# Attention by pairs of heads in column and row halves of TensorE's array, with four score banks and two banks for the turned probabilities

## The reference, cut to what matters

```python
def softmax_attend(q, k, v, scale):
    s = jnp.einsum('bqhd,bkhd->bhqk', q, k, preferred_element_type=jnp.float32) * scale
    p = jax.nn.softmax(s, axis=-1).astype(v.dtype)
    return jnp.einsum('bhqk,bkhd->bqhd', p, v)
```

## Time and profile before

| | |
|---|---|
| median of 3 runs | 2400.22 us (2400.1 to 2400.34) |
| the profiled execution's own time | 2396.24 us |
| its span | 2394.4 us |
| PE busy with matmuls | 2138.0 us (89% of the span) |
| PE busy with weight loads | 1714.3 us |
| DVE busy | 1188.7 us |
| ACT busy | 857.6 us |
| mean granted clock of TensorE | 0.944 of full speed |
| scores L1130 | 192 PE instructions, of 96 matmuls |
| turns L1139 | 320 PE instructions |
| values L1152 | 320 PE instructions, of 160 matmuls |

### The profile page before, as it was taken

The page is one execution under the profiler, slowest core; times in us unless marked ns, Lnnn a source line. Parts: engine busy times, 40 slices in busy tenths (PEclk is TensorE's granted clock), DMA queues, the critical chain, the costliest instruction groups (busy, mean ns, idle before and its releaser), DMA issues.

```text
span 2394.4 us, 32007 instructions
## 1 busy us (share of the span) xinstructions
PE 2138.0 (89%) x12456; PEld 1714.3 (72%) x12456; DVE 1188.7 (50%) x2027; ACT 857.6 (36%) x1362; POOL 188.9 (8%) x186
## 2 busy tenths in 40 slices
PE   4999899799989999998898989889987579986998
PEld 2777458347757777775874746879977579986997
DVE  5322444454454333334433464655667576666665
ACT  3422342253242222222433434343344633333343
POOL 0000000000110003003000000200330320011001
PEclk8999899899999999998998989989989889998998
DMA  8426104012534554545381322855541345542553
GB/s 287 138 80 200 53 18 152 11 53 88 176 105 159 172 180 141 199 151 175 117 261 53 124 58 76 272 187 182 181 140 62 115 131 165 180 159 88 168 184 106
DMA packets 280855, 332.06 MB, mean 139 GB/s; under 512 B 13286, under 2 KB 229788, under 8 KB 280604
## 3 DMA queue, kind: packets, MB, share of 16 engines
q1 hardware_dynamic: 268704, 323.05, 41.3%
q10 hardware_dynamic: 12028, 7.31, 1.2%
HBM read 329.29 MB, written 1.05 MB: 138 GB/s over the span
## 4 chain that ended last, share of the span: by engine, by line
PE 70%; issue 10%; DVE 10%; ACT 4%; DMA 3%; POOL 2%; ACTq 0%; POOLq 0%; DVEq 0%
PE ps L467 17%; PE ps L468 17%; PE ps L469 17%; PE ps L1152 3%; PE ps L344 3%; PE ps L1130 2%; DVE SL L431 2%; PE ps L1139 1%; ACT SH L425 1%; DVE SM L1223 1%; PE ps L354 1%; PE ps L1299 1%; DVE RSTD L839 1%; PE ps L1305 1%; DMA RAW<-in_ffn_w 1%
## 5 line engine op out<-in xcount | busy, mean ns | idle before, releaser
L431 DVE TENSOR_TENSOR SL<-RAW,SH 128x1024 fp32r<-128x1024 f32 (+3 forms) x460 | 530.8, 1157 | 899.8 <-ACT SH L425 897.8
L425 ACT ACTIVATE SH<-RAW 128x1024 fp32r<-128x1024 f32 (+3 forms) x460 | 447.8, 980 | 1067.7 <-PE ps L469 920.6
L467 PE MATMUL ps<-AH,SH 128*128 128x256 f32 (+1 forms) x2048 | 674.1, 329 | 79.3 <-DVE AL L871 30.3
L468 PE MATMUL ps<-AL,SH 128*128 128x256 f32 (+1 forms) x2048 | 665.7, 325 | 0.0
L469 PE MATMUL ps<-AH,SL 128*128 128x256 f32 (+1 forms) x2048 | 664.7, 325 | 0.0
L467 PEld LDWEIGHTS ps<-AH,SH 128*128 128x128 f32 x2048 | 399.2, 195 | 143.7 <-issue 49.4
L469 PEld LDWEIGHTS ps<-AH,SL 128*128 128x128 f32 x2048 | 398.9, 195 | 29.3
L468 PEld LDWEIGHTS ps<-AL,SH 128*128 128x128 f32 x2048 | 399.3, 195 | 27.3
L467 PE MATMUL ps<-HH,SH 128*128 128x256 f32 (+1 forms) x992 | 310.1, 313 | 8.2 <-DVE HL L741 4.4
L469 PE MATMUL ps<-HH,SL 128*128 128x256 f32 (+1 forms) x992 | 309.0, 311 | 0.0
L468 PE MATMUL ps<-HL,SH 128*128 128x256 f32 (+1 forms) x992 | 308.2, 311 | 0.0
(11 more groups left out here) (237 smaller groups left out, 2207.6 us busy)
## 6 DMA issues: line engine op xcount, KB each, us to landing
SIDE<-in_w_mod SPq DMA_DIRECT2D x45, 2048.0 KB, 8.1
RAW<-in_ffn_w SPq DMA_DIRECT2D x64, 1024.0 KB, 5.4
RAW<-in_w_in SPq DMA_DIRECT2D x44, 1024.0 KB, 5.8
RAW<-in_w_ffn_gate SPq DMA_DIRECT2D x22, 1024.0 KB, 10.1
RAW<-in_w_ffn_up SPq DMA_DIRECT2D x22, 1024.0 KB, 5.9
RAW<-in_w_ffn_down SPq DMA_DIRECT2D x16, 1024.0 KB, 5.6
RAW<-in_w_branch SPq DMA_DIRECT2D x24, 512.0 KB, 3.5
RAW<-in_w_out SPq DMA_DIRECT2D x8, 1024.0 KB, 5.5
```

What stands on the lines that cost most here:

```text
L425: e.activation(SH[:, m, 0:kt, :], RAW[p][:, 0:kt, o:o + P], ACT.Copy).then_inc(K.up("weight_high"), 1)
L431: e.tensor_tensor(SL[:, m, 0:kt, :], RAW[p][:, 0:kt, o:o + P], SH[:, m, 0:kt, :].bitcast(F32), ALU.subtract).then_inc(K.up("weight_low"), 1)
L467: e.matmul(ps, SH[:, m, k, :], xh, start=k == 0, stop=False)
L468: e.matmul(ps, SH[:, m, k, :], xl, start=False, stop=False)
```

## The change

- The steps are put in another order: the two heads of a pair alternate, so that step n and step n+1 (n even) are the same query tile of an even and of an odd head. In `na` their scores then lie in the upper and in the lower 64 rows of the array.
- Scores use four banks, ps6, ps7, ps2 and ps3 (columns of SM for maxima and sums are also four deep). Turns use two banks, ps5 and ps1. Outputs of values use ps4 and ps0 in turn, one for each pair of heads.
- The values are computed once for four steps: for each 128 keys, one matmul of the even head into the partitions 0 to 63 and one of the odd head into the partitions 64 to 127 of the same bank.
- The orders on PE, ACT and DVE are rewritten in twos, as below. The scaling of the probabilities stays on DVE and stays in place.
- The section waits at its start for all eight banks, and the sections behind it wait for its last readers of all eight.

The number of instructions of each kind is unchanged. The diff, cut to its core:

```diff
+        SCORES = (6, 7, 2, 3)
+        TURNED = (5, 1)
+        OUT = (4, 0)
-            self.steps = [(s, h, qt) for s in range(streams) for h in range(HEADS) for qt in range(2)]
+            self.steps = [(s, 2 * hp + j, qt) for s in range(streams) for hp in range(HEADS // 2) for qt in range(2)
+                          for j in range(2)]
+            self.pairs = len(self.steps) // 4
...
-            for b in (4, 5, 6, 7):
+            for b in range(8):
                 reader, count = K.bank[b]
                 e.wait_ge(sem[reader], K.value(reader, count))
...
             def scores(n):
-                if n >= 2:
-                    e.wait_ge(sem["exp_done"], K.at("exp_done", n - 1))
+                if n >= 4:
+                    e.wait_ge(sem["exp_done"], K.at("exp_done", n - 3))
...
             def turn(n):
                 e.wait_ge(sem["probs_ready"], K.at("probs_ready", n + 1))
-                if n:
-                    e.wait_ge(sem["turned_copied"], K.at("turned_copied", n))
+                if n >= 2:
+                    e.wait_ge(sem["turned_copied"], K.at("turned_copied", n - 1))
...
+            def values(pair):
+                s, h, _ = self.steps[4 * pair]
+                e.wait_ge(sem["turned_copied"], K.at("turned_copied", 4 * pair + 4))
+                if pair >= 2:
+                    e.wait_ge(sem["branch_low"], K.at("branch_low", pair - 1))
+                o = PS[self.OUT[pair % 2]]
                 for j in range(tiles):
-                    ins = e.matmul(o, V[:, c0 // P + j, 64 * h:64 * h + 64], PTS[:, g % 2, j, :], start=j == 0,
-                                   stop=j == tiles - 1)
+                    for i in range(2):
+                        ins = e.matmul(o[64 * i:64 * i + 64, 0:256], V[:, c0 // P + j, 64 * (h + i):64 * (h + i) + 64],
+                                       PTS[:, i, j, :], start=j == 0, stop=j == tiles - 1)
...
-            scores(0)
-            scores(1)
-            for n in range(n_steps):
-                if n + 2 < n_steps:
-                    scores(n + 2)
+            for n in range(4):
+                scores(n)
+            for n in range(0, n_steps, 2):
                 turn(n)
-                if n >= 2 and n % 2 == 0:
-                    values(n // 2 - 1)
-            values(n_steps // 2 - 1)
-            K.bank[4] = ("branch_low", K.s("branch_low") + n_steps // 4)
-            K.bank[5] = ("turned_copied", K.s("turned_copied") + n_steps)
-            K.bank[6] = K.bank[7] = ("exp_done", K.s("exp_done") + n_steps)
+                turn(n + 1)
+                if n >= 4 and n % 4 == 0:
+                    values(n // 4 - 1)
+                if n + 4 < n_steps:
+                    scores(n + 4)
+                    scores(n + 5)
+            values(self.pairs - 1)
+            for b in self.OUT:
+                K.bank[b] = ("branch_low", K.s("branch_low") + self.pairs)
+            for b in self.TURNED:
+                K.bank[b] = ("turned_copied", K.s("turned_copied") + n_steps)
+            for b in self.SCORES:
+                K.bank[b] = ("exp_done", K.s("exp_done") + n_steps)
...
         def act(self, e, K):
-            for n in range(n_steps + 1):
+            for n in range(0, n_steps + 2, 2):
                 if n < n_steps:
                     exp(n)
-                if n >= 1:
+                    exp(n + 1)
+                if n >= 2:
+                    turned(n - 2)
                     turned(n - 1)
-                if n >= 5 and (n - 5) % 4 == 0:
-                    out((n - 5) // 4)
+                if n >= 6 and n % 4 == 2:
+                    out((n - 6) // 4)
...
         def dve(self, e, K):
-            for n in range(n_steps + 1):
+            for n in range(n_steps + 2):
                 if n < n_steps:
                     maximum(n)
-                if n >= 1:
-                    normalise(n - 1)
-                if n >= 6 and (n - 6) % 4 == 0:
-                    out((n - 6) // 4)
+                if n >= 2:
+                    normalise(n - 2)
+                if n >= 9 and n % 4 == 1:
+                    out((n - 9) // 4)
```

More of the change, by code:

```diff
@@ L1110, in qk, with scores_of @@
             return Q96[0:96, h, q0:q0 + P], K96[0:96, h, c0:c1]
+        def scores_of(self, n):
+            c0, c1 = self.keys(self.steps[n][0])
+            return PS[self.SCORES[n % 4]][:, 0:c1 - c0]
         def pe(self, e, K):
@@ L1125, in scores @@
                 s, h, qt = self.steps[n]
-                if n >= 2:
-                    e.wait_ge(sem["exp_done"], K.at("exp_done", n - 1))
-                q, k = self.qk(s, h, qt)
-                c0, c1 = self.keys(s)
[L1130 to L1135, removed]
-                if n:
-                    e.wait_ge(sem["turned_copied"], K.at("turned_copied", n))
-                for j in range((c1 - c0) // P):
-                    ins = e.transpose(PS[5][:, j * P:(j + 1) * P], PR[:, n % 2, j * P:(j + 1) * P], IDENT)
-                ins.then_inc(K.up("probs_turned"), 1)
@@ L1142, in values @@
[L1142 to L1147, removed]
+                if n >= 4:
+                    e.wait_ge(sem["exp_done"], K.at("exp_done", n - 3))
+                q, k = self.qk(s, h, qt)
+                e.matmul(self.scores_of(n), q, k, start=True, stop=True).then_inc(K.up("scores_done"), 1)
@@ new lines, in turn @@
+            def turn(n):
+                c0, c1 = self.keys(self.steps[n][0])
+                e.wait_ge(sem["probs_ready"], K.at("probs_ready", n + 1))
+                if n >= 2:
+                    e.wait_ge(sem["turned_copied"], K.at("turned_copied", n - 1))
+                for j in range((c1 - c0) // P):
+                    ins = e.transpose(PS[self.TURNED[n % 2]][:, j * P:(j + 1) * P], PR[:, n % 2, j * P:(j + 1) * P],
+                                      IDENT)
+                ins.then_inc(K.up("probs_turned"), 1)
@@ L1169, in outputs @@
+            for b in self.TURNED:
+                K.bank[b] = ("turned_copied", K.s("turned_copied") + n_steps)
+            for b in self.SCORES:
+                K.bank[b] = ("exp_done", K.s("exp_done") + n_steps)
         def outputs(self, pair):
             s = self.steps[4 * pair][0]
-            return pair % 4, slice(s * SEQ, (s + 1) * SEQ), slice(256 * (pair % 2), 256 * (pair % 2) + 256)
+            return pair % 4, slice(s * SEQ, (s + 1) * SEQ), PS[self.OUT[pair % 2]][:, 0:256]
         def act(self, e, K):
@@ L1176, in exp @@
             def exp(n):
-                s, h, qt = self.steps[n]
-                c0, c1 = self.keys(s)
+                c0, c1 = self.keys(self.steps[n][0])
                 e.wait_ge(sem["max_done"], K.at("max_done", n + 1))
@@ L1181, in exp @@
                     e.wait_ge(sem["probs_turned"], K.at("probs_turned", n - 1))
-                e.activation(PR[:, n % 2, 0:c1 - c0], PS[6 + n % 2][:, 0:c1 - c0], ACT.Exp,
-                             bias=SM[:, n % 2:n % 2 + 1], accum_out=SM[:, 2 + n % 2:3 + n % 2]) \
-                    .then_inc(K.up("exp_done"), 1)
+                e.activation(PR[:, n % 2, 0:c1 - c0], self.scores_of(n), ACT.Exp, bias=SM[:, n % 4:n % 4 + 1],
+                             accum_out=SM[:, 4 + n % 4:5 + n % 4]).then_inc(K.up("exp_done"), 1)
             def turned(n):
@@ L1214, in maximum @@
                 s, h, qt = self.steps[n]
-                c0, c1 = self.keys(s)
                 e.wait_ge(sem["scores_done"], K.at("scores_done", n + 1))
-                ps = PS[6 + n % 2]
+                ps = self.scores_of(n)
                 if self.kind == "na" and s == 0:
```

37 lines of the change are left out of this document (18 added, 19 removed).

## The result

The changed kernel takes 2434.72 us (median of 4 runs, 2427.44 to 2443.25), against 2400.16 us (4 runs, 2398.88 to 2400.34) for the kernel before, run beside it. The ratio is 1.0142, with a 95% interval from 1.012 to 1.0163: slower by 1.4%. The forecast was 2443 us with a range from 2409 to 2484.

A forecast was written before the change was run, and what follows sets the result against it. PE was taken to bound the kernel before. Stage changes of +43 us took the profiled 2396.24 us to 2439; the runs' median stands 4 us above, giving 2443 us, range 2409 to 2484.

The forecast's parts named there:

- The circle: Attention: DVE waits for scores queued behind turns and values; `na` pair, 512 keys, 2.4 GHz, 12.31 us against 10.86.
- The halves: Values in Attention: column halves overlap, so a pair's 16 instructions take 1.87 us; bounds 1.87 to 3.74.
- Row halves: Scores of two heads in `na`: may overlap, bounds 0 to 0.86 us for a pair of scores; nothing counted.
- The clock: `na` mostly at 1.2 GHz, priced 14 to 46 us; `mla` at 2.4 GHz except part of the 256-key steps.
- the first rival: Attention: the ring of waits closes but the clock stays up; +3.5 us, 2404 us, chance 0.14.
- The third case: `mla` loses its clock too: pairs of 14.6 instead of 9.9 us, 2478 us in all, chance 0.15.
- The sum: Four attention stages: `na` +26.5 and +15, `mla` +1.1 and -1.4, +2 for low clock; in all +43 us.
- The 2 us for the unit behind each `na`: After each `na`: the unit behind starts at the low clock, plus 2 us in each layer.
- The rises of the clock: `na`: a short rise after each run of values, worth 0.8 us each; -2.5 in layer 0, -1.5 in layer 1.
- a shorter tail: End of each attention: one run of values in halves instead of two whole ones, -1.9 us with 512 keys.
- The handover wait: End of each attention: the next unit's first matmul waits in ps0 for YH and YL, about 0.95 us, four times.
- The rival on the other side: Attention: DVE or PE work is the bound, not the ring of waits; faster, 2331 us, chance 0.05.

The follow-up runs named there:

- kernel with fillers: Changed kernel plus one unread score matmul on PE ahead of each turn, in both attentions; 2417.34 us, ratio 1.0079 against the kernel before.
- kernel with swapped outputs: Changed kernel with the two output banks of the values, ps4 and ps0, exchanged; 2434.46 us, ratio 1.013 against the kernel before.
- the one with the filler in `na` alone: Changed kernel plus unread score matmuls ahead of turns, only in `na` and from the second two steps on; 2422.61 us, ratio 1.0086.
- both handover edits: Changed kernel with the two output banks exchanged and ps0 counted free after the last pair but one; 2434.18 us, ratio 1.0136.
- scores-first kernel: Changed kernel with the scores of steps n+4 and n+5 put ahead of turns n and n+1; 2354.81 us, ratio 0.9813 against the kernel before.
- the halves in series: Values of one head issued whole before the other's: 2448.53 us in the changed kernel, 2372.91 us with the scores also ahead of the turns.
- the old queues and new values: Changed kernel with PE, ACT and DVE orders of the kernel before, keeping new head order, banks and column halves; 2378.59 us, ratio 0.9919.

## Why the prediction was right, and where it was off

**What bounds the kernel.** PE bound the kernel before and was no longer the bound after, as forecast: its busy share in the first `na` fell from 95 to 70%, the wait of DVE for the score stands in every second step (3.21 us at 1.2 GHz, 1.61 in `mla`), and the turn waits for the scaling.

**The circle.** Its sums for 512 keys, and for 256 at the low clock, held; each is made of differences in the timeline of before:

| two steps, us | predicted | measured | where |
|---|---|---|---|
| `na` 512 keys, 2.4 GHz | 5.22 and 7.09 with values | 5.21 and 7.09 | kernel with fillers |
| `na` 512 keys, 1.2 GHz | 6.64 and 10.24, less 0.8 for a rise | 6.62 and 9.28 | 275.66, 282.28, 291.56 |
| `na` 256 keys, 1.2 GHz | 3.7 and 5.6 | 3.60 and 5.51 | waits of L1236 at 340.98, 344.58, 350.09 |
| `mla` 512 keys, 2.4 GHz | 4.08 and 6.17 | 4.09 and 6.15 | 515.05 to 525.29 |

For the third line, the maxima that waited for a score of 256 keys:

```profile
340.98 0.42 DVE L1236 TENSOR_REDUCE SM<-ps 128x1 f32<-128x256 f32 x1 [3.84 <-PE ps L1138]
344.58 0.42 DVE L1236 TENSOR_REDUCE SM<-ps 128x1 f32<-128x256 f32 x1 [1.60 <-PE ps L1138]
350.09 0.42 DVE L1236 TENSOR_REDUCE SM<-ps 128x1 f32<-128x256 f32 x1 [3.84 <-PE ps L1138]
```

For 256 keys at 2.4 GHz the sum was 2.90 us, and 3.91 with values. `mla` shows 2.64 (553.20 to 555.84) and 3.85 (563.47 to 567.32), and once 4.99, where the clock was 0.66 (555.84 to 560.83). The 2.90 had been made from rows of `na`.

**The halves.** Taken as 1.87 us for 16 instructions, from a row with column quarters; measured 1.95 with the tail of the last, as 8 had 1.94. Right.

**Row halves.** I counted nothing for them. They overlap (last section). In the changed kernel I see no gain from it, for the reason given: DVE needs the second score later, and the first of each two comes no sooner (280.17 to 282.28 is 2.11 us, as in the earlier trace rows). No run took the overlap away, so this is read from the timeline and not tested.

**The clock.** Taken as mostly 1.2 GHz in `na`: 0.59 and 0.61 are right, against the first rival. For `mla` I took 2.4 GHz but for part of the 256-key steps: 0.98 and 1.00 in this execution. The third case (`mla` loses its clock too) is not borne out by this execution: `mla` has as many turns as `na` and kept its clock. The Trainium skill's rule on transposes that stood beside it (TensorE: Matmul & The Clock Gate, PE-mode transpose) therefore does not decide here: 96 transposes in each of the two stages, 0.59 in the one and 0.98 in the other. But the case is not quite dead either. The profiled executions of the kernel with swapped outputs and of the one with the filler in `na` alone show 73.15 and 73.17 us at 0.88 in `mla` of layer 0, against 66.80 at 1.00 in the one with both handover edits:

```profile
511.19:584.34 73.15, 58.08 (x257) 29.76 (x257) 35.40 (x104) 37.70 (x105) 0.00 (x0) 0.88 0.13 44
```

```profile
510.34:577.14 66.80, 50.72 (x256) 26.79 (x256) 34.86 (x103) 37.58 (x104) 0.00 (x0) 1.00 0.14 48
```

The four runs of the changed kernel fall in two groups, 2427 and 2429 us with a mean granted clock of 0.926 and 0.927, and 2440 and 2443 us with 0.920 and 0.918. The profile of the changed kernel is from the first group only. That the second group lost `mla`'s clock as these two did is likely, but no profile of it was taken; and `mla` can give only 4 to 6 of the 14 us between the groups. The rest is open; between the profiles of the changed kernel and of the one with swapped outputs, 13.1 us apart, 4.1 are `mla` of layer 0 and 9.6 lie outside of the four stages.

**The sum.** The terms by stage, for the profiled execution: `na` layer 0 forecast +26.5, measured +21.8; `na` layer 1 +15 and +11.2; `mla` layer 0 +3.1 (with the low clock in part of it) and +2.4; `mla` layer 1 -1.4 and +0.5. In all +43 and +35.8. The steps that were mis-sized:
- The 2 us for the unit behind each `na`, which starts at the low clock. From the end of `na` to the start of `mla` it was 145.70 us before (340.00 to 485.70) and is 144.77 after (363.22 to 507.99); in layer 1 it is 100.8 both times. Nothing was lost there in this execution. That is 4 of the 7 us. The kernels with swapped outputs and with both handover edits, whose `na` ran at the same low clock, took 147.87 and 147.29 us for the first of these two, so for layer 0 a cost like mine isn't excluded.
- The rises of the clock. I gave 0.8 us for each run of values. But the first steps of 256 keys ran at the high clock in good part (scores of 0.70 us at 321.98, 325.30 and 331.64, and of 1.23 from 339.72 on). The first `na` came out 2.7 us shorter than my sum without the term above, that of layer 1 by 1.8.
- `mla` in layer 1. I counted -1.4, the wait at its end included; it came out 1.9 higher. The timelines of the two kernels show where its +0.5 comes from. From the first score to the values that complete the first pair it takes 14.26 us (1469.51 to 1483.77) where it took 12.24 (1436.46 to 1448.70), since one more round of the circle now lies ahead of the first values: +2.0. The next two pairs cost +0.6 and the tail, its wait included, gives back 2.2. The sum names a shorter tail for this stage and no start.

The handover wait was sized at 0.95 us and measured at 1.03 in the wait and 1.1 in the distance.

I had put the profiled execution at 2439 us; it took 2427.44. Of the nearly 12 us between, 7.2 are the sum and 4.7 the scatter outside of the stages. From there to the median I had put 4 us, and it was 7.3 (2434.72 less 2427.44), so that the forecast ended 8 us high. That this second miss took 3 us off the first is luck.

**The rival on the other side**, a bound by the work of DVE or PE, was placed rightly: it decides if the score reaches DVE before the second normalisation ends, and the moved calls do just that. I had worked out 7.1 us for a pair and 2331 us. The scores-first kernel gives 7.83 and 2354.8. PE has 7.00 us of work in that pair, more than DVE, and the clock is not yet up throughout (0.91 and 0.78 over the `na` stages). With the halves in series as well, PE has 0.91 us more of work in a pair and the pair takes 0.90 us more (8.73, values at 283.86 and 292.59), with DVE's work as it was. So even with the order mended PE's work counts in full, and DVE alone is not the bound. The Trainium skill's rule beside this rival, that after tiling the engines that empty PSUM may become the bound (TensorEngine Tiling (Array Packing), PSUM Bottleneck), is therefore not borne out by this kernel, though DVE comes near it: it is busy for 6.78 of the 7.83 us.

## What to carry to other kernels

When a change makes an engine's work shorter and reorders the queues, walk once around the queues before counting the work: for each engine's next instruction, name what it waits for and what stands ahead of that in its queue. If the walk comes back to where it began within one iteration, the time of an iteration is the sum of the latencies on the way. Here that sum could be read off a timeline of the kernel before to two hundredths of a microsecond, for the rounds of 512 keys at a steady clock. Four score banks didn't open this circle; issuing the next scores ahead of the turns did, and it was worth 80 us for three lines. And price the clock with it: in `na` the gaps went with a granted clock of 0.59 and 0.61, which stretched the very parts that are on the circle, while in `mla` much the same circle ran at 0.98 and 1.00.

## What the runs showed of the hardware that was not expected

- **Row halves overlap fully.** Two scores of two heads in row halves, four instructions of 64 rows and 512 columns, take 2.08 us at 1.2 GHz and 1.13 us at 2.4 GHz (273.55 and 290.40 above). One score, two instructions, took 2.07 and 1.12.
- **Halves issued in series overlap in part.** Eight matmul instructions of one column half, then eight of the other, take 2.86 us at 2.4 GHz; eight of one half alone took 1.94 and sixteen interleaved 1.95. With four and four the order costs nothing: 1.09 us in series and 1.08 interleaved.
- **Work that nobody reads can shorten a kernel.** The fillers took 17 us off the changed kernel, with the clock in `na` at 0.88 and 0.81 in place of 0.59 and 0.61 (2434.7 to 2417.3, in two sessions with the kernel before at 2400.2 and 2399.6).
- **Some of the kernels scatter more.** The four runs of the changed kernel spread over 15.8 us, and the longer ones had the lower mean granted clock; those of the kernel with the old queues and new values spread over 14.9, those with the scores first over 3.7 and, with the values in series, 3.0. The kernel before spread over 1.5 us beside the changed one, and over 10.4 us at most in another session (2397.64 to 2408.07). With four runs each this is a hint, and no cause of it was tested.
